# Splitting all twelve weight slots of a one-group pass into high and low words (WHOLE = () in place of (5, 7))

## The reference, cut to what matters

```
logits = (xt @ w_router) + b_router                  # (1024, 32)
top_vals, top_idx = lax.top_k(logits, 4); gates = softmax(top_vals)
# the tokens of each expert are gathered in blocks of 128
def expert_block(xblk, e):
    h = xblk @ w1[e] + b1[e]                         # 1024 -> 2048
    return clamped_swiglu(h) @ w2[e] + b2[e]         # 1024 -> 1024
out[token] += y * gate                               # scatter-add of four experts per token
```

## Time and profile before

| | us |
|---|---|
| median of 3 runs | 2288.44 (2286.68 to 2290.86) |
| the profiled execution | 2293.3 |
| its span | 2291.6 |
| TensorE matmul busy | 2175.5 (95%) |
| VectorE busy | 1422.4 (62%) |
| ScalarE busy | 1094.1 (48%) |
| expert passes | from about 590 to the end |

### The profile page before, as it was taken

One profiled execution on the slowest core, in us unless ns is written; L12 is line 12 of the kernel. 1 busy time (PEld: TensorE's weight loads), 2 busy tenths in 40 slices (PEclk: granted clock), 3 DMA queues, 4 the chain that ended last, 5 costly groups with the idle time before them and its releaser, 6 DMA issues.

```text
span 2291.6 us, 31520 instructions
## 1 busy us (share of the span) xinstructions
PE 2175.5 (95%) x9748; PEld 1609.1 (70%) x9749; DVE 1422.4 (62%) x2152; ACT 1094.1 (48%) x1602; POOL 227.6 (10%) x208
## 2 busy tenths in 40 slices
PE   6999988996999999999999999999999999999997
PEld 4443776443578877776787878787778877887885
DVE  3342573334775677768767575768786657667665
ACT  3241452112464465556555454546565445445444
POOL 2000200002210011011101010110100110101001
PEclk9999997996999999999999999999999999999998
DMA  7000402002795589869958586858997658658556
GB/s 254 1 0 19 157 1 74 28 28 88 275 362 195 187 277 332 289 205 348 343 177 322 182 297 198 290 183 326 353 335 265 204 174 297 196 177 315 181 182 220
DMA packets 203190, 477.62 MB, mean 208 GB/s; under 512 B 14744, under 2 KB 20952, under 8 KB 203089
## 3 DMA queue, kind: packets, MB, share of 16 engines
q1 hardware_dynamic: 185662, 437.95, 52.7%
q0 software_dynamic: 17424, 39.17, 7.5%
q10 hardware_dynamic: 66, 0.02, 0.0%
HBM read 468.73 MB, written 32.11 MB: 219 GB/s over the span
## 4 chain that ended last, share of the span: by engine, by line
PE 73%; DVE 8%; issue 7%; ACT 6%; DMA 4%; DVEq 1%; POOLq 1%; ACTq 0%; POOL 0%; SPq 0%
PE ps L1107 15%; PE ps L1109 15%; PE ps L1108 15%; PE ps L878 7%; PE ps L1032 5%; DMA out<-y,idx_cur 4%; DVE w_lo L1576 3%; PE ps L1168 3%; ACT w_hi L752 2%; PE ps L1143 2%; PE ps L1161 1%; PE ps L1101 1%; PE ps L983 1%; PE ps L951 1%; DVE hm L1636 1%
## 5 line engine op out<-in xcount | busy, mean ns | idle before, releaser
L1576 DVE TENSOR_TENSOR w_lo<-ring,w_hi 128x1024 fp32r<-128x1024 f32 x692 | 815.5, 1219 | 182.1 <-ACT w_hi L752 178.7
L752 ACT ACTIVATE w_hi<-ring 128x1024 fp32r<-128x1024 f32 x692 | 696.4, 1055 | 295.9 <-PE ps L1109 277.1
L1107 PE MATMUL ps<-w_hi,xT_hi 128*128 128x512 f32 x1288 | 512.6, 398 | 20.5 <-ACT y L778 15.2
L1109 PE MATMUL ps<-w_hi,xT_lo 128*128 128x512 f32 x1288 | 503.3, 391 | 0.0
L1108 PE MATMUL ps<-w_lo,xT_hi 128*128 128x512 f32 x1288 | 503.1, 391 | 0.0
L1107 PEld LDWEIGHTS ps<-w_hi,xT_hi 128*128 128x128 f32 x1288 | 242.4, 188 | 81.8 <-issue 32.5
L1107 PE MATMUL ps<-w_hi,actT_hi 128*128 128x512 f32 x720 | 289.4, 402 | 0.0
L1109 PE MATMUL ps<-w_hi,actT_lo 128*128 128x512 f32 x720 | 281.9, 392 | 0.0
L1108 PE MATMUL ps<-w_lo,actT_hi 128*128 128x512 f32 x720 | 281.2, 390 | 0.0
L1108 PEld LDWEIGHTS ps<-w_lo,xT_hi 128*128 128x128 f32 x1288 | 242.2, 188 | 55.2 <-issue 4.5
L1109 PEld LDWEIGHTS ps<-w_hi,xT_lo 128*128 128x128 f32 x1288 | 242.2, 188 | 51.7
(11 more groups left out here) (262 smaller groups left out, 1997.4 us busy)
## 6 DMA issues: line engine op xcount, KB each, us to landing
ring<-in_w SPq DMA_DIRECT2D x390, 1024.0 KB, 7.2
xh<-in_x SPq DMA_DIRECT2D x4, 2048.0 KB, 15.7
work<-in_w_out SPq DMA_DIRECT2D x1, 4096.0 KB, 12.9
token_rows<-uT POOLq DMA_DIRECT2D x8, 512.0 KB, 2.9
out<-xh SPq DMA_DIRECT2D x8, 512.0 KB, 2.7
work<-in_w_in SPq DMA_DIRECT2D x2, 1536.0 KB, 18.4
uT<-in_w_mem_kv SPq DMA_DIRECT2D x1, 2048.0 KB, 13.7
ring<-in_w_in SPq DMA_DIRECT2D x1, 1536.0 KB, 18.7
```

The source lines that it names most:

```text
L752: act_e.activation(w_hi[h % SPLIT][:, :, :], part(h), ACT.Copy).then_inc(hi_ready, counted(h, whole))
L1107: pe.matmul(acc, hi, whi, start=first, stop=False)
L1109: return pe.matmul(acc, lo, whi, start=False, stop=last)
L1576: return dve.tensor_tensor(lo, x, hi.bitcast(F32), ALU.subtract)
```

## The change

`WHOLE` is empty, so in a one-group pass slots 5 and 7 are split and multiplied like the others.

```
@@ -52,7 +52,7 @@
 RAW = 6
 SPLIT = 8
 LEAD = 6
-WHOLE = (5, 7)
+WHOLE = ()
 AHEAD_OOB = 1 << 20
```

## The result

| | us |
|---|---|
| changed kernel, median of 4 runs | 2351.98 (2346.93 to 2354.68) |
| kernel before, median of 4 runs | 2288.66 (2286.68 to 2290.86) |
| ratio | 1.0273, 95% interval 1.0258 to 1.0288 |
| span of the profiled execution, before and after | 2291.6 and 2345.2 |

The kernel became 2.7% slower, 63 us by the medians. In the two profiled executions the loop over passes grew from 1701.4 to 1761.3 us (first matmul of the first pass to the end), 59.8 us; the part ahead of the loop was 6.2 us shorter in the second one, so the spans differ by 53.6 us only. The change doesn't touch that part: it has the same instructions in every kernel here, and takes 583.8 to 592.3 us in their traces.

A forecast was written before the change was run, and what follows sets the result against it. In calm one-group passes TensorE was level with a loop through scatter, `idx_cur`, VectorE and the last transposes. Forecast: 2288.4 plus 62.2 for loop growth and 20 for the clock, 2370 us; range 2343 to 2396.

The forecast's parts named there:

- The loop grows: One-group passes: VectorE's added subtractions between the L1570 release and `take_alo(2)` lengthen the loop by 3.58 us per pass.
- Rival 4: ScalarE comes late: returned buffer waits put one 1.055 us copy more into the loop; 2389 us, chance 0.05.
- 4.54 - 0.59 - 0.37: VectorE, L1570 to `take_alo(2)`: four subtractions, less the waits for `gelu(1)` and slot 8's `w_hi`; 3.58 us.
- I take no gain: Scatter's landing behind the last matmul: possibly some 0.4 us sooner than its 8.99 us wait, but counted as nothing.
- The clock: TensorE, about 3.7 us idle before the last transposes: half clock afterwards costs 2.7 us per fall, +20 us in all.
- about half: Share of the 17 counted one-group passes in which TensorE's clock was expected to fall.
- what an earlier `combine(0)` gives back: Deduction from the clock's cost in the passes where it falls, included in the +20 us.
- The pass that never waited: The one one-group pass without a wait at L1570: VectorE has slack, so it gets TensorE's -1.4 us.
- the late one: The one-group pass where `act(0)` ended just before 1885.30: end at 1914.6 against 1911.9, +2.7 us.
- 62.2: Sum over the 19 one-group passes before the clock: 17·3.58 = 60.9 us, plus two special passes; +62.2 us.
- Rival 3: TensorE stays the bound: `idx_cur` 5.0 us earlier puts VectorE's new work beside TensorE's, 27 us gained; 2262 us, chance 0.04.

The follow-up runs named there:

- e1: Only slot 7 split in addition to the kernel before, slot 5 left whole; 2305.34 us, ratio 1.0082.
- e2: Only slot 5 split in addition to the kernel before, slot 7 left whole; 2335.06 us, ratio 1.0199.
- e3: Changed kernel with `make_idx` (L1570 wait included) moved behind `split_lo(6)` in one-group passes; 2266.67 us, ratio 0.9904.
- e6: Changed kernel with 8 extra constant matmuls, and SyncE waiting for `idx_cur` before loading slot 8; 2314.62 us, ratio 1.0128.
- e5: Changed kernel with 8 extra constant-operand matmuls ahead of the last activation transposes in one-group passes; 2347.02 us, ratio 1.0262.
- e7: Changed kernel with SyncE waiting for `idx_cur` before loading slot 8, no extra matmuls; 2323.23 us, ratio 1.0156.

## Why the prediction was right or wrong

**The loop and its place: right.** "The loop grows" was the step on which all rested, and e1, e2 and e3 show it: 16 us, 46 us and -23 us against the kernel before, for the same kind of work before or behind one wait. TensorE's waits at L1143 rose from 11.0 to 59.7 us as foretold (some 65). Two-group passes stayed at 71.5 us. VectorE's wait at L1570 was to stay at about 85 us and fell from 88.4 to 74.3; that is 0.8 us per pass, not the 4 us that would have spoken against the loop. Rival 4, a late ScalarE, is out by the trace: VectorE waits for it in the stretch for 0.65 us, and for 1.62 us before.

**The size of the growth: 3.58 us foretold, 3.03 measured.** The step that failed in size is "4.54 - 0.59 - 0.37", which left out short pauses that a full queue closes: the start of `make_onehot` came some 0.27 us sooner behind its predecessor, the instruction behind `idx_next` 0.09 us, and both waits that it named were in truth 0.09 us longer than their idle column, because neighbouring records overlap. 17 times 0.55 are 9 us of the miss.

**The scatter: "I take no gain" was wrong by 8 us.** L1570 came 8.2 us sooner in sum, 7.0 of it in the nine passes behind one-group passes. The likely cause is that a slower end of the pass puts a weight load ahead of the scatter. e6 shows that loads beside the scatter delay it; that their order does is argued from e5.

**The clock: +20 us foretold, +15.1 us measured in the last stretch of the passes.** The gap was foretold as 3.7 us and is 3.38. The clock fell at the last transposes in 15 of the 19 passes, more often than "about half", but in nine of them for 3.4 us instead of 6.8, and it cost at most 1.7 us there, not 2.7. The prediction took some 3 us off in sum for what an earlier `combine(0)` gives back. It was more, as the next pass's first matmul shows: before, it waits 0.83 us for ScalarE's `y`; in all passes of the changed kernel whose clock fell at the last transposes and that another pass follows, it doesn't wait (the line at 1726.77 above). So the first 0.83 us that slower matmuls add in a pass cost nothing. A fall of 6.8 us, of which about 1 us lay in the idle time before, cost 1.6 to 1.7 us, one of 3.4 us 0.3 to 0.6. The price was right only in sum, and by luck: more passes paid, and each paid less. And its cost cannot be added to the rest: in e5 it was taken away whole, and the time fell by 5 us in place of 15.

**The pass that never waited and the late one: -0.6 and +1.9 us,** foretold -1.4 and +2.7.

Together 62.2 + 20 = 82 us were foretold, and 59.8 us came in the loop of the profiled execution, 63 us by the medians. The misses are 9 us at VectorE's pauses, 8 us at the scatter and 5 us at the clock. Rival 3 (TensorE stays the bound, faster) asked for a release 5.0 us earlier, and it came at most 1.9 us earlier in a pass. But its other half is true: e3 moves the work instead of the release, and the kernel is then 1% faster, 23 us where the rival counted 27.

## What to carry to other kernels

Idle time on an engine is worth nothing to work that is queued behind the wait that makes it; find the wait, and add the work ahead of it or move the wait (2352 us and 2267 us are the same instructions). When two chains meet in a loop through a DMA, a gain on one of them moves the DMA against the other traffic and against the other engines' work: check where each transfer is issued, and beside what, before and after, because here it gave back 14 us once and 48 us once. A wait's share on the page names the place; what it costs follows only from the stretch between two fixed points of a pass, compared in both traces.

## What the runs showed of the hardware that was not expected

- Issuing the indirect scatter took up to 5.87 us instead of 1.62 under an unbroken run of VectorE instructions with two SBUF operands, and ended 1.58 us behind the first one without.
- The scatter of 128 rows landed 6.3 to 8.3 us after its start in the changed kernel where the nearest weight load was issued at least 0.6 us ahead of it (12 of 13 scatters behind one-group passes; one took 10.0), and 9.2 to 10.4 us in e5, where that load was issued 0.2 to 0.3 us behind its start (all but one, which took 7.1). In the kernel before the load was as close behind, and the scatter landed after 8.0 to 9.4 us, so its place is not all that counts. Holding the loads back brought GpSimd's wait in one-group passes that follow on each other to about 7.2 us from about 10.
- TensorE's granted clock fell to 0.50 around idle times of 2.3 to 3.4 us in 15 of the 19 one-group passes of the changed kernel and not in others (in e7 one gap of 3.39 us kept the full clock). At half clock split matmuls started 0.43 us apart.
